# A hybrid decoder step: one-hots split between two engines, a buffer of its own for one tile, values in two column strips, and another spread of gather rows

## The reference, cut to what matters

```
def block(args):
    hb, eb, gb = args
    act = jax.nn.gelu(jnp.einsum('tkd,td->tk', u_tab[eb], hb))
    return jnp.einsum('tk,tkd->td', gb * act, v_tab[eb])
```

## Time and profile before

| | us |
|---|---|
| median of 3 runs | 4615.84 (4615.41 to 4619.94) |
| the profiled execution | 4618.78 |
| its span | 4617.1 |
| PE busy | 4451.5 (96%) |
| DVE busy | 2713.8 (59%) |
| POOL busy | 983.3 (21%) |
| ACT busy | 414.3 (9%) |
| mean granted clock of PE | 0.983 |

### The profile page before, as it was taken

The page is one execution under the profiler, slowest core; times in us unless marked ns, Lnnn a source line. Parts: engine busy times, 40 slices in busy tenths (PEclk is TensorE's granted clock), DMA queues, the critical chain, the costliest instruction groups (busy, mean ns, idle before and its releaser), DMA issues. The chain is left out here.

```text
span 4617.1 us, 50491 instructions
## 1 busy us (share of the span) xinstructions
PE 4451.5 (96%) x20466; PEld 3698.0 (80%) x20466; DVE 2713.8 (59%) x4629; ACT 414.3 (9%) x910; POOL 983.3 (21%) x747
## 2 busy tenths in 40 slices
PE   8999999999999999999999899999999999999993
PEld 7888888888767676667776679999999988888983
DVE  4434500017688788645556569866788655545556
ACT  1111100001111111110000110010000000000000
POOL 1000000000112313023334332323233222222222
PEclk9999999999999999999999999999999999999997
DMA  4444444555579879658899799989999999999996
GB/s 171 140 140 140 162 155 146 180 174 183 200 263 350 323 264 391 233 206 353 360 364 392 302 360 380 378 339 405 372 383 380 353 421 389 395 356 420 424 422 249
DMA packets 269674, 1387.04 MB, mean 300 GB/s; under 512 B 46721, under 2 KB 53121, under 8 KB 141330
## 3 DMA queue, kind: packets, MB, share of 16 engines
q0 software_dynamic: 99344, 720.05, 39.2%
q1 hardware_dynamic: 170098, 663.77, 39.0%
HBM read 1341.95 MB, written 40.29 MB: 299 GB/s over the span
## 5 line engine op out<-in xcount | busy, mean ns | idle before, releaser
L413 PE MATMUL ps<-X,BIG 128*128 128x320 f32 (+1 forms) x5632 | 1405.4, 411 | 4.8 <-DVE X L1484 4.2
L413 PEld LDWEIGHTS ps<-X,BIG 128*128 128x128 f32 x5632 | 1074.4, 191 | 318.8 <-issue 16.0
L1000 DVE CUSTOM_DVE_ANT_0 RING<-RING,CUR 128x2048 f32<-128x2048 f32 x302 | 689.6, 2291 | 371.3 <-DMA RING<-in_peer_u,table 193.6
L1008 DVE SCALAR_TENSOR_TENSOR CUR<-RING,wexp,CUR 128x2048 f32<-128x2048 f32 x304 | 714.6, 2351 | 311.0 <-DMA RING<-in_peer_v,table 179.9
L766 PE MATMUL ps<-X,RA 128*128 128x240 f32 x4096 | 844.5, 367 | 1.6 <-DMA RA<-in_uT 1.3
L766 PEld LDWEIGHTS ps<-X,RA 128*128 128x128 f32 x4096 | 774.9, 191 | 54.7 <-DMA RA<-in_uT 3.1
L2085 POOL DMA_INDIRECT RING<-in_peer_v,table x224 | 326.4, 1457 | 954.7 <-DVE CUR L1008 765.6
L413 PE MATMUL ps<-BIG 128*128 128x256 f32 (+1 forms) x2048 | 503.7, 407 | 12.8 <-DVE BIG L1470 10.6
L2085 POOL DMA_INDIRECT RING<-in_peer_u,table x222 | 331.5, 1493 | 841.7 <-DVE hidden L1000 575.1
L413 PEld LDWEIGHTS ps<-BIG 128*128 128x128 f32 x2048 | 389.5, 191 | 122.4 <-DVE BIG L1470 12.1
L786 PE MATMUL ps<-BIG,RA 128*128 128x240 f32 x2048 | 440.8, 369 | 15.1 <-DMA RA<-in_peer_v 14.5
(11 more groups left out here) (315 smaller groups left out, 2899.1 us busy)
## 6 DMA issues: line engine op xcount, KB each, us to landing
BIG<-in_w_in_b SPq DMA_DIRECT2D x128, 1024.0 KB, 5.8
RA<-in_uT SPq DMA_DIRECT2D x256, 512.0 KB, 8.2
RA<-in_peer_v SPq DMA_DIRECT2D x256, 512.0 KB, 9.6
BIG<-in_w_gb_b SPq DMA_DIRECT2D x32, 1024.0 KB, 5.3
BIG<-in_w_ga_b SPq DMA_DIRECT2D x32, 1024.0 KB, 5.0
BIG<-in_w_gla_o_b SPq DMA_DIRECT2D x32, 1024.0 KB, 5.2
BIG<-in_w_mix_b SPq DMA_DIRECT2D x32, 1024.0 KB, 5.8
BIG<-in_w_q_b SPq DMA_DIRECT2D x32, 1024.0 KB, 7.2
```

The lines of the kernel that those rows point to most:

```text
L413: last = pe.matmul(bank[:, 0:n], w(k, j * P, P), src[:, k, 0:n], start=(k == 0), stop=(k == kt - 1))
L1000: row_used.on(dve.tensor_tensor_reduce(out=row, in0=row, in1=h2cur[0:n, :], scale=1.0, scalar=0.0, op0=ALU.mult, op1=ALU.add, accum_out=hi ...
L1008: row_used.on(dve.scalar_tensor_tensor(out=cur[0:n, :], in0=row, scalar=wexp[0:n, par, k:k + 1], in1=cur[0:n, :], op0=ALU.mult, op1=ALU.ad ...
```

## The change

1. The sets of one-hots with gates are made on ACT (`gated_onehots`, an absolute value of the difference and then a relu of the gate minus twice that), eight activations of 128x128 per set, in place of DVE's four L1518. DVE makes the one-hots without gates for four tokens in one instruction in place of two.
2. The 16-token tile has a query buffer of its own, in the place of the one-hots; its query is loaded eight rows before the tile begins, and the next tile's query follows directly. The move of the routing results is made in 16 small DMAs (8 before), four rows after the routing of group 1 is over.
3. The products L595 of even k go to partitions 0 to 63, those of odd k to 64 to 127 of the same bank; ACT copies both, and DVE adds them (`sample_values`).
4. The number of gather rows at each place differs: in `gates` of group 1 there is one more place, and the others are larger; in the U stage the paces are 3.4 and 3.9 in place of 3.8 and 3.2, and after the routing 3.9 in place of 4.2, in the G stage 4.1 in place of 4.2.

```diff
-MOVE_AT = (1, 3, "u", 4)
+ENDS = 16
-U_PACE = 4.2
+U_PACE = 4.1
+        v_odd = part_of(RA, 3584, DV)[0:NS, :]
+        own_gates = holes[:, 15, 0:HP * TOPK]
+        query = (h2cur, h2cur, h2cur, part_of(BIG, 32768 - D, D))
-        ohs = [[part_of(BIG, NB * ND + 1024 * q + 512 * i, 2, 2, P) for i in range(2)] for q in range(2)]
+        ohs = [part_of(BIG, NB * ND + 1024 * q, 2, 4, P) for q in range(2)]
...
             def sample_intra(h):
+                pe.wait_ge(*vs_ready.at(h))
...
                         for k in range(KT):
-                            last = pe.matmul(bank[0:NS, 0:PAIR], normT[g][:, k, span(2)], w(k, 0, PAIR), start=(k == 0),
-                                             stop=(k == KT - 1))
+                            at = NS * (k % 2)
+                            last = pe.matmul(bank[at:at + NS, 0:PAIR], normT[g][:, k, span(2)], w(k, 0, PAIR),
+                                             start=(k < 2), stop=(k >= KT - 2))
...
+                    pe.wait_ge(*onehot_ready.at(q))
+                    pe.wait_ge(*oh_gated.at(q))
                     for n in range(4):
-                        if n % 2 == 0:
-                            pe.wait_ge(*onehot_ready.at(q, n // 2))
...
+            def sample_values(h):
+                dve.wait_ge(*v_ready.at(1, h, 1, 1))
+                vs_ready.on(dve.tensor_tensor(vt[0:NS, 2, :], vt[0:NS, 2, :], v_odd, ALU.add), h)
...
+                if g:
+                    spare((0, "gates2"), 9.6)
                 merge_a(g, 0)
                 for i in range(1, D // PAIR):
                     if g:
-                        spare((i, "gates1"), 15.0)
+                        spare((i, "gates1"), 28.8 if i == 1 else 17.5)
                     merge_b(g, i)
                     if g:
-                        spare((i, "gates2"), 15.0 if i < D // PAIR - 1 else 0.0)
+                        spare((i, "gates2"), 17.5 if i < D // PAIR - 1 else 0.0)
...
-                    for i in range(2):
-                        dve.tensor_scalar(ohs[q % 2][half][:, 0, i, :], iota128[:, :], sel[:, 0, i:i + 1],
-                                          sel[:, 2, i:i + 1], ALU.is_equal, ALU.mult)
-                    onehot_ready.on(dve.tensor_tensor(
-                        ohs[q % 2][half][:, 1, :, :], iota128[:, :].unsqueeze(1).to_broadcast([P, 2, P]),
-                        sel[:, 1, :].unsqueeze(2).to_broadcast([P, 2, P]), ALU.is_equal), q, half)
+                onehot_ready.on(dve.tensor_tensor(
+                    ohs[q % 2][:, 1, :, :], iota128[:, :].unsqueeze(1).to_broadcast([P, 4, P]),
+                    sel.unsqueeze(2).to_broadcast([P, 4, P]), ALU.is_equal), q)
...
                 if b < G_AT - 1:
-                    paced(work_1, 3.8)
-                    paced(work, U_PACE if routed.n == ROUTED else 3.2)
+                    paced(work_1, 3.4)
+                    paced(work, 3.9)
...
             for i in range(ENDS):
-                spare(("end", i), 45.0)
+                spare(("end", i), 30.0)
...
+            def gated_onehots(q):
+                if q == 0:
+                    act.wait_ge(*selT_ready.now())
+                    act.wait_ge(*own_moved.at("gates", PH - 1))
+                elif q > 1:
+                    act.wait_ge(*ps_done.at("g", q - 2))
+                for n in range(4):
+                    c = q % 32 * 4 + n
+                    dst = ohs[q % 2][:, 0, n, :]
+                    i, j = 2 * (q // 32) + c // 64, c % 64
+                    oh_step.on(fn(dst, iota128[:, :], ACT.Abs, scale=-1.0, bias=selT[:, 0, i, j:j + 1]), q, n)
+                for n in range(4):
+                    c = q % 32 * 4 + n
+                    dst = ohs[q % 2][:, 0, n, :]
+                    i, j = 2 * (q // 32) + c // 64, c % 64
+                    act.wait_ge(*oh_step.at(q, n))
+                    ins = fn(dst, dst, ACT.Relu, scale=-2.0, bias=selT[:, 2, i, j:j + 1])
+                oh_gated.on(ins, q)
...
             def query_load(t):
-                if t:
-                    pool.wait_ge(*y_g.at(before_tile[t]))
-                else:
+                if t == 0:
                     pool.wait_ge(*normT_ready.at(1, KT - 1))
                     pool.wait_ge(*x2_stored.at(0))
+                elif t == 3:
+                    pool.wait_ge(*ps_done.at("g", ND // 4 - 1))
+                else:
+                    pool.wait_ge(*y_g.at(t - 1))
...
                 t = row_list[m][0]
-                if row_list[m] == MOVE_AT:
+                if m == seen["routing_over"] + 4:
                     own_move()
                 gather(m)
...
                 if t and m == first_row[t] + 2:
-                    query_load(t)
+                    if t == 1:
+                        query_load(1)
+                    y_store(before_tile[t])
+                    if t == 3:
+                        query_load(2)
+                if m == first_row[3] - 8:
+                    query_load(3)
```

More of the change, by code:

```diff
@@ L1000, in gather_rows @@
                             row_used.on(dve.tensor_tensor_reduce(
-                                out=row, in0=row, in1=h2cur[0:n, :], scale=1.0, scalar=0.0, op0=ALU.mult,
+                                out=row, in0=row, in1=query[t][0:n, :], scale=1.0, scalar=0.0, op0=ALU.mult,
                                 op1=ALU.add, accum_out=hidden[0:n, par, k:k + 1]), m)
@@ L1329, in head @@
                 taps(g, h, (TAPS, 21)[g], TAPS)
+                if g:
+                    sample_values(h)
                 silu_r(g, h, 0)
@@ L1656, in v_keep @@
                     act.wait_ge(*ps_done.at("vs", g, h, p))
+                    if (h, p) == (0, 0):
+                        act.wait_ge(*qk_zeroed.at(1))
+                    fn(v_odd[:, cols], banks.of("vs", g, h, p)[NS:P, 0:PAIR], ACT.Copy)
                     v_ready.on(fn(vt[0:NS, 2, cols], banks.of("vs", g, h, p)[0:NS, 0:PAIR], ACT.Copy), g, h, p, 1)
```

66 lines of the change are left out of this document (36 added, 30 removed).

## The result

The changed kernel takes 4577.6 us (median of 4 runs, 4572.7 to 4586.4), the kernel before 4615.6: ratio 0.9924, 95% interval 0.9907 to 0.994. It is 38 us faster. The forecast was 4542 us, with a range of 4512 to 4575. The time lies 2.6 us above the range, and the gain is half of the 73 us forecast.

A forecast was written before the change was run, and what follows sets the result against it. PE was taken as the bound up to 4534 us, the gather rows after that. The terms -61, -5, -15, +3, +3 and +2 sum to -73 from 4618.8, so 4545.8, stated as 4542 us; range 4512 to 4575.

The forecast's parts named there:

- The end: End of the kernel: the gather finishes before PE, so the first norm sum loses its 59.2 us wait and half clock: -61 us.
- the query loads: V stage, around the 16-token tile: two query loads leave the gather's path, so the gather ends 20 to 30 us earlier.
- The U stage: U stage: DVE's lead covers most of ten more rows, leaving a short PE wait at the first one-hots: +2, between 0 and 8.
- The G stage: G stage: with gated one-hots on ACT, PE's waits for one-hots and the half clock behind go: -15, between -5 and -16.
- ACT's cover: G stage: ACT finishes each block's gated one-hots 2.5 to 3 us before PE wants them, costed at 0.
- rival D: G stage: ACT's gated one-hots outlast the block at 1.0 us per activation: +50, about 4666 us; chance 0.07.
- The heads: Heads: the strips show 7 of 28 us, and half clock after new waits costs about 10: +3, between -28 and +12.
- The gates: Gates of group 1: 22 more rows just fit PE's slack, in some steps not: +3, between 0 and 10.
- The V tiles: V stage: part of PE's 25 us of waits for V tiles goes once the gather ends earlier: -5, between 0 and -15.
- Rival B: Denser rows make DVE late: gates 10, heads 12, U 8, mixing 4, V tiles 0; +31, about 4574 us; chance 0.13.
- mixing: Mixing stage: the row counts at each place hardly differ: 0, within 4 us.

The follow-up runs named there:

- e12: The changed kernel with the 16-token tile's query back in the common buffer, both query loads placed as before: 4578.1 us, ratio 0.9927.
- e1: The changed kernel with the row paces of the kernel before in the U and G stages: 4555.1 us, ratio 0.9874.
- e8: The kernel before with all row places and paces of the changed kernel, the move in its 8 DMAs: 4578.3 us, ratio 0.9924.
- e2: The changed kernel with the gates stage's row places of the kernel before: 4590.4 us, ratio 0.9951.
- e6: The kernel before with only the 22 more gather rows in the gates stage, and the routing move 20 rows later: 4547.0 us, ratio 0.9849.
- e7: e1 with the gated one-hots made on DVE again: 4567.6 us, ratio 0.9903.
- e13: e9 with the gated one-hots made on DVE again: 4544.8 us, ratio 0.9855.
- e4: The changed kernel with the gated one-hots made on DVE again: 4578.9 us, ratio 0.9927.
- e5: e1 with 4.8 us of gather rows before the taps of each head of group 1 in place of 12.0: 4555.8 us, ratio 0.9878.
- e9: e1 with the 16-token tile's query back in the common buffer, both query loads placed as before: 4534.2 us, ratio 0.9846.
- e10: e9 with 7.2 us of gather rows before the taps of each head of group 1 in place of 12.0: 4535.9 us, ratio 0.9845.
- e11: The same kernel as e1, measured again: 4556.6 us, ratio 0.9878.
- e14: e9 with the sample values computed in one strip again: 4543.0 us, ratio 0.9856.
- e3: The changed kernel with the sample values computed in one strip again: 4582.2 us, ratio 0.9934.

## Why the prediction was wrong, point by point

**The end.** Right in size and cause: -59.2 of wait and -1.8 of clock. The gather's end, forecast for 4417 to 4427, came at 4488 (last row). Its pace from the V stage on is 189 steps in 822 us (last row 4488.4, row 487 at 3666.0), 4.35 us each, near the 4.27 used, which makes 15 us; it began 26 us later, because DVE was late; and the 20 to 30 us of the query loads did not come off: without the own buffer (e12) the last row ends at 4487.2.

**The U stage. This is the step that failed**: "Ten rows of 4.27 us are 43, of which that lead covers most", +2 taken, bounds 0 and 8. It was +38. The place was right, and the term was mis-sized, by four things. The row behind which the stage's rows are counted stands at the same place of DVE's program in both kernels, as row 263 before and as row 283 after. Here it is with the first one-hots of the kernel before, and then in the changed kernel, whose first one-hots are shown above at 3231.03:

```profile
2738.77 2.28 DVE L1000 CUSTOM_DVE_ANT_0 RING<-RING,CUR 128x2048 f32<-128x2048 f32 x1
...
3193.47 0.60 DVE L1518 TENSOR_SCALAR BIG<-iota,X 128x128 f32<-128x128 f32 x2
```

```profile
2750.53 2.29 DVE L1005 CUSTOM_DVE_ANT_0 RING<-RING,CUR 128x2048 f32<-128x2048 f32 x1 [0.32 <-DMA RING<-in_peer_u,table]
```

All waits of DVE in the changed kernel's stage, to be read against the earlier trace rows:

```profile
DVE RING L1005 <- DMA RING<-in_peer_u,table: 57.9, 32, 7.1
DVE CUR L1013 <- DMA RING<-in_peer_v,table: 39.7, 21, 5.6
```

First, there are twelve rows more and not ten: 92 stand there in the trace before, and 104 now. Second, a row costs 4.60 us in this stage. The kernel before takes 452 us from 2741.1 to 3193.5, waits 29 of them for ACT, and uses the other 423 for 92 rows; the changed kernel takes 478 us for 104. The 4.27 is the V stage's; here DVE is busy for 137 of the 478 us with other steps between the rows, most of them the routing's. So twelve rows are 55 us. Third, the lead covers 29 of them, more than half but not most: the changed kernel's DVE has no wait for ACT left. That leaves 26. Fourth, DVE is 12 us later at the start (2752.8 against 2741.1) while PE starts at the same time. Its rows in front, 20 more, had cost DVE that time, and the sum had it at nothing. 26 + 12 are the 38. My own sum already left 43 - 26 + 4 = 21 us, and I wrote +2. e1 and e8 show the cause from both sides. The parts can't be told apart to the last microsecond: e2 starts the stage at 2740.1 and still loses 33 us, at 4.65 us a row.

**The G stage.** -14.4 us measured, -15 forecast, for the wrong reason. The length of the stage in all kernels:

| gated one-hots | pace | G stage, us |
|---|---|---|
| DVE | 4.2 | 461.2 (before), 451.8 (e6), 446.7 (e7), 451.8 (e13) |
| DVE | 4.1 | 447.9 (e4), 446.4 (e8) |
| ACT | 4.2 | 445.4 (e1), 445.7 (e5), 446.0 (e9), 446.6 (e10), 446.8 (e11), 445.6 (e14) |
| ACT | 4.1 | 446.8 (after), 446.8 (e2), 447.9 (e3), 447.9 (e12) |

The gates' rows alone bring 9 of the 14 us (e6), and with the pace 4.1 all of them are there without ACT's one-hots (e8). With that pace 100 rows stand in the stage, and 102 did before, where the text ahead of the prediction says as many as before. At 4.35 us a row the two are 9 us of DVE's time. Why rows taken in front of the U stage shorten the G stage is not shown, and ACT's one-hots in the kernel before, without the other rows, were not run: at its 461.2 us they may be worth more than the 1 to 6 us seen at the pace 4.2. DVE's busy time in the stage fell by 67 us (376.9 to 309.9), not by the 95 worked out, because instructions that follow each other overlap: the six of one set took 1.78 us (3200.98 to 3202.76) and not 2.28. ACT's cover was as forecast, and rival D did not come: 0.40 us per activation, no wait of PE for them.

**The heads.** Forecast +3 within -28 and +12, measured -5 (e3), -6 on the faster base (e14), by the start of the U stage. The mechanism was right: the third `r` product waits 4.55 us in head 1, at the granted clock of 0.66, and DVE's chain decides (e5). The stalls were put too high: four waits of 12.1 us in all, where the sum had 7 + 3 x 5 = 22.

**The gates.** Forecast +3, measured 0: from 1943 to 2594 PE is busy for 632.7 us before and 633.9 after, and e2, without the rows, has 633.5.

**The V tiles.** Forecast -5: the waits went from 25.0 to 27.8 us. That the gather ends 62 us ahead of PE did not help, because most of these waits (23 of the 28 us) stand between 3700 and 4100, around the 16-token tile, and not at the end of the gather.

**The range and the rivals.** Rival B named the right place, the U stage, among others, and put at most 8 us on it; its 4574 is close to the measured time, but by luck, since its 26 us in heads, gates and mixing did not come (the table has -0.4 for them together). With the term read from the stage itself (12 x 4.60 - 29 = 26 in place of 2, and of the bound of 8) the forecast would have stood at 4566 and the range ended at 4593; with DVE's 12 us at the start the forecast is 4578.

## What to carry to other kernels

Price work by the pace of the stage into which it goes, not of another: the 4.60 us stood in the trace of the kernel before, beside the 4.27 that I used. An engine's wait shows how much more work it can take there, and no more: 29 us here, of 55. When work is moved forward to shorten a tail, count at each later meeting point how much stands in front of it, and how late the engine already comes; and don't round away what your own sum leaves. Here 22 more rows in one stage with room gave 64 us (e6), and the other paces took 31 of it back (e8). Taking 67 us of work from an engine that waits for transfers gave 0 to 6 us here; first find out whether the engine or its transfers are late.

## What the runs showed of the hardware

- Two strips of 64 columns that add into different partitions of one bank ran beside each other: 32 records in 3.67 us, against 7.12 in one strip.
- An activation of 128x128 with a pointer as bias took 0.40 us here, as absolute value and as relu, and loaded no table between gelus; the exponential between gelus did, 1.28 us each way.
- Two query loads that are issued ahead, beside running gathers and V tiles, went with 374 GB/s in place of 399 in a stretch of 160 us at one set of row paces (e11 against e9; e1 has 386), and with 388 and 393 at another (changed kernel and e12). It was not tried why.
